# RWKV / delta-rule trunk on one core: layer ends by token half, the norm's scale and offset moved, full-row products

## The reference

```python
for layer in range(2):
    if layer == 0:     # 8 heads of stick-breaking attention (128 wide), 16 RWKV-7 heads (64 wide)
        h = concatenate([attention(...), rwkv7_group(...)]) @ ev_w_out
    else:              # gated delta rule, 32 value heads, chunks of 64
        h = gated_deltanet(x @ od_w_in, ...) @ od_w_out
    x = layer_norm(ALPHA * x + h, ln1_g[layer], ln1_b[layer])
    x = layer_norm(ALPHA * x + square(relu(x @ mlp_w1)) @ mlp_w2, ln2_g[layer], ln2_b[layer])

def layer_norm(x, g, b):
    mu, var = mean(x), mean((x - mu)**2)
    return (x - mu) * rsqrt(var + 1e-5) * g + b
```

## Time and profile before

| | |
|---|---|
| median of 3 runs | 2956.7 us (2956.69 to 2959.77) |
| the profiled execution | 2961.85 us |
| its span, first to last instruction | 2960.2 us |
| mean granted clock of PE | 0.993 |
| PE busy | 2903.2 us (98%) |
| PE weight loads busy | 2531.9 us (86%) |
| DVE busy | 1857.0 us (63%) |
| ACT busy | 1446.9 us (49%) |
| read from HBM | 488.89 MB, 166 GB/s over the span |

### The profile page before, as it was taken

How to read it: one execution, slowest core, us unless ns; L and a number is a source line. 1 busy time by engine, 2 the same in 40 slices (tenths; PEclk the granted TensorE clock), 3 DMA queues, 4 the chain that set the end, 5 groups by cost and what they waited for, 6 DMA issues and landing times.

```text
span 2960.2 us, 53673 instructions
## 1 busy us (share of the span) xinstructions
PE 2903.2 (98%) x20900; PEld 2531.9 (86%) x20900; DVE 1857.0 (63%) x2604; ACT 1446.9 (49%) x2248; POOL 14.9 (1%) x31
## 2 busy tenths in 40 slices
PE   8999999899999999999999999999999999999998
PEld 8888897788888888889999988999887888888886
DVE  5777776755555545565677766577767546455556
ACT  5545544344444434435666765466744434344442
POOL 0000000000000000000000000000000000000000
PEclk9999999999999999999999999999999999999999
DMA  7333344465555555544344444544445555555554
GB/s 246 118 117 115 116 125 149 173 218 192 187 191 192 186 191 188 194 157 136 129 143 144 143 136 144 192 136 146 140 178 179 191 192 185 194 190 192 192 186 149
DMA packets 156762, 493.77 MB, mean 167 GB/s; under 512 B 15600, under 2 KB 50416, under 8 KB 155296
## 3 DMA queue, kind: packets, MB, share of 16 engines
q1 hardware_dynamic: 153488, 475.33, 48.2%
q0 software_dynamic: 2800, 14.94, 1.3%
q10 hardware_dynamic: 288, 0.79, 0.1%
HBM read 488.89 MB, written 2.10 MB: 166 GB/s over the span
## 4 chain that ended last, share of the span: by engine, by line
PE 91%; DVE 5%; ACT 2%; issue 1%; DMA 0%; DVEq 0%; ACTq 0%; SPq 0%
PE pp L433 45%; PE mp L433 11%; PE pp L417 8%; PE mp L417 8%; PE pp L419 4%; PE mp L419 4%; DVE wl L1442 1%; PE mp L867 1%; PE mp L836 1%; PE mp L821 1%; PE mp L873 1%; PE mp L813 1%; ACT wh L935 0%; DMA raw<-in_w_dram 0%; PE mp L787 0%
## 5 line engine op out<-in xcount | busy, mean ns | idle before, releaser
L1442 DVE TENSOR_TENSOR wl<-raw,wh 128x1024 fp32r<-128x1024 f32 (+1 forms) x936 | 1100.9, 1183 | 783.2 <-ACT wh L935 782.2
L935 ACT CAST wh<-raw 128x1024 fp32r<-128x1024 f32 (+1 forms) x936 | 944.8, 1018 | 890.8 <-PE pp L433 287.1
L433 PE MATMUL pp<-aT,wh 128*128 128x256 f32 x3680 | 705.1, 292 | 12.1 <-DVE wl L1442 12.1
L433 PEld LDWEIGHTS pp<-aT,wh 128*128 128x128 f32 x3680 | 575.8, 192 | 28.4 <-issue 16.9
L433 PE MATMUL pp<-aT,wl 128*128 128x256 f32 x1840 | 522.0, 284 | 0.0
L417 PE MATMUL pp<-aT,wh 128*128 128x512 f32 x1024 | 365.4, 401 | 0.0
L417 PE MATMUL mp<-aT,wh 128*128 128x512 f32 x1024 | 360.8, 398 | 0.0
L433 PE MATMUL pp<-wh,hTh 128*128 128x512 f32 x896 | 357.5, 399 | 3.0 <-DVE wl L1442 1.5
L433 PEld LDWEIGHTS pp<-aT,wl 128*128 128x128 f32 x1840 | 353.7, 192 | 0.0
L433 PE MATMUL pp<-wh,hTl 128*128 128x512 f32 x896 | 349.8, 390 | 0.0
L433 PE MATMUL pp<-wl,hTh 128*128 128x512 f32 x896 | 349.5, 390 | 0.0
(11 more groups left out here) (323 smaller groups left out, 3082.4 us busy)
## 6 DMA issues: line engine op xcount, KB each, us to landing
raw<-in_w_dram SPq DMA_DIRECT2D x800, 512.0 KB, 3.3
raw<-in_w_dram SPq DMA_DIRECT2D x136, 384.0 KB, 3.5
ws<-in_ln_dram POOLq DMA_DIRECT2D x8, 1024.0 KB, 7.5
xres<-in_x_dram POOLq DMA_DIRECT2D x1, 2048.0 KB, 8.7
out_dram<-xres SPq DMA_DIRECT2D x8, 256.0 KB, 2.0
ws<-in_lora_dram POOLq DMA_DIRECT2D x8, 192.0 KB, 4.4
xres<-in_xt_dram POOLq DMA_DIRECT2D x2, 512.0 KB, 6.7
ws<-in_c_dram POOLq DMA_DIRECT2D x1, 576.0 KB, 6.4
```

The costliest lines, as they stand in the source:

```text
L433: last = mm(o, lhs, rhs, start=opens and m == 0, stop=end and kk == 1 and m == 2, skip_group_check=True)
L935: nc.scalar.copy(wh[:, q % RING, :, 0:width], raw[:, q % LAND, :, 0:width]).then_inc(S("hi_ready"), 1)
L1442: tt(wl[:, q % RING, :, 0:width], raw[:, q % LAND, :, 0:width], f(wh[:, q % RING, :, 0:width]), ALU.subtract).then_inc(S("lo_ready"), 1)
```

## The change

It has four parts.

1. **Layer ends by token half.** `last_panel` on DVE (the former `tail`, generalised) adds and takes the statistics of the last panel for t = 0 as soon as PE has finished that half of the last unit (`ends`, semaphore `tail`), then for t = 1. `new_x` now normalises without scale and offset (one operation for a piece, `ts` with mean and 1/std), the first 512 columns in pieces of 256. The tiles of PE, ACT and DVE are now 256 columns of both token halves (two k-tiles). ACT applies scale and offset as it reads the transposed block, since they are per-partition numbers there (`lnT`, a new small input, loaded by POOL at the start), into the staging `scaled_x` (two halves of `hid`), copies the high part from it, and DVE subtracts for the low part. In the first tile DVE does the odd block (`odd`) and the two k-tiles are handed over singly. PE's first half unit waits for the first k-tile alone.
2. **Late scale and offset of the residual.** `residual` does `xres * lng + lnb` on DVE, in eight pieces of two operations, in later steps of the MLP's first body, or in the gate steps of layer 1. `lng` and `lnb` move to other places in the work space.
3. **Unread products.** `keep_clock` issues 16 products of 256 columns before the first transposes of each layer end and 6 behind the second tile. Nobody reads them.
4. **Tables and shapes.** Out-projection 0 goes 6+2 instead of 7+1, with 24 units under the last `mix0` and 8 behind. L556 uses all 128 rows of `lw` (the others are zero), L677 the full 128 columns of keys, and the rows not wanted are not read.

```diff
-HOPS_GATES = 4 * (4,) + (5,) + 9 * (3,)
+HOPS_GATES = 8 * (2,) + (5,) + 9 * (3,)
-HOPS_MLP = 4 * (2,) + 56 * (1,)
+HOPS_MLP = 64 * (1,)
+HOPS_E = 2 * (1,) + 31 * (2,)
+HOPS_G = 2 * (1,) + HOPS_GATES[1:]
...
+        scaled_x = [r2(hid[:, i * WIDE:(i + 1) * WIDE], a=UK) for i in range(2)]
...
@@ POOL
+            pool.dma_start(lnT[:, :, :, :], lnt.rearrange("p (k s c) -> p k s c", k=3, s=2)).then_inc(S("masks_in"), 16)
...
@@ PE, unit
+                    if ends and j == 0:
+                        last.then_inc(S("tail"), 1)
...
@@ PE, new_x
+                def keep_clock(count):
+                    if k == 2:
+                        pe.wait_ge(S("evacuated"), B_L1 + 1)
+                    for _ in range(count):
+                        mm(pp[0][:, 0:T] if k == 2 else mb[3][:, 0:T], hTh[:, 0, 0:P], hTh[:, 0, :], start=True, stop=True,
+                           skip_group_check=True)
                 def turn(r):
-                    c, t = divmod(r, TT)
-                    pe.wait_ge(S("x_ready"), 8 * (k - 1) + r + 1)
-                    if 8 * k + r >= 12:
-                        pe.wait_ge(S("xlo"), 8 * k + r - 3)
-                    for e in range(4):
-                        last = nc.tensor.transpose(mb[r % 4][:, e * P:(e + 1) * P],
-                                                   xres[:, t, (4 * c + e) * P:(4 * c + e + 1) * P], ident)
+                    if r >= 4:
+                        pe.wait_ge(S("xhi"), 9 * k + r - 3)
+                    for t in range(TT):
+                        if r >= 2 or t == 0:
+                            pe.wait_ge(S("x_ready"), 18 * (k - 1) + (4 + 2 * (r // 2) if r >= 2 else r + 1))
+                        else:
+                            pe.wait_ge(S("x_ready"), 18 * (k - 1) + r + 3)
+                        for e in range(UK):
+                            bank = mb[2][:, 0:T] if r == 0 and e else mb[r % 4][:, e * T:(e + 1) * T]
+                            last = nc.tensor.transpose(bank[:, t * P:(t + 1) * P],
+                                                       xres[:, t, (UK * r + e) * P:(UK * r + e + 1) * P], ident)
                     last.then_inc(S("xT" if r < 7 else "x_transposed"), 1)
-                for y, tiles in enumerate((range(0, 4), range(4, 6), range(6, 8), ())):
-                    for r in tiles:
-                        turn(r)
-                    pe.wait_ge(S("xlo"), 8 * k + 2 * y + 2)
+                keep_clock(16)
+                turn(0)
+                turn(1)
+                keep_clock(6)
+                for y in range(UNITS + 1):
+                    if 0 < y <= 6:
+                        turn(y + 1)
+                    pe.wait_ge(S("xlo"), 9 * k + y)
                     yield
...
@@ PE, mix0
-                mm(mb[0][:, T:2 * T], lw[0:32, 2, :], loT[0:32, 2, :], start=False, stop=True,
+                mm(mb[0][:, T:2 * T], lw[:, 2, :], loT[:, 2, :], start=False, stop=True,
...
-                            last = mm(mb[0][half(1 - hf), 0:P], KR[:, hf, 0, t, :], st_in, start=True, stop=True,
-                                      skip_group_check=True)
+                            turned_keys = KR[:, hf, :, :, :].rearrange("p w t c -> p (w t c)")[:, t * HC:t * HC + P]
+                            last = mm(mb[0][:, 0:P], turned_keys, st_in, start=True, stop=True, skip_group_check=True)
...
-            drive(late(blocks(P_OUT0, B_OUT0, "A", H, (0, 1, 0, 1), WIDE, per=7), 6, "mix0_out", GROUPS - 1), 28, 0,
-                  mix0(GROUPS - 1, False), HOPS0Z)
+            drive(blocks(P_OUT0, B_OUT0, "A", H, (0, 1, 0, 1), WIDE, per=6), 24, 0, mix0(GROUPS - 1, False), HOPS0Z)
             pe.wait_ge(S("mix0_out"), GROUPS)
-            drive(blocks(P_OUT0, B_OUT0 + 4, "A", H, (0, 1, 0, 1), WIDE, per=1, u0=28, k0=14), 4, 28)
+            drive(blocks(P_OUT0, B_OUT0 + 4, "A", H, (0, 1, 0, 1), WIDE, per=2, u0=24, k0=12, ends=31), 8, 24)
...
@@ ACT, new_x
+                def part(r, e):
+                    c = UK * r + e
+                    return go(scaled_x[r % 2][:, e, :], mb[r % 4][:, e * T:(e + 1) * T], ACT.Identity,
+                              scale=lnT[:, k - 1, 0, c:c + 1], bias=lnT[:, k - 1, 1, c:c + 1])
+                def high(r):
+                    y = scaled_x[r % 2]
...
+                    if r >= 2:
+                        act.wait_ge(S("xlo"), 9 * k + r - 1)
+                    st(part(r, 0))
+                    if r:
+                        st(part(r, 1))
+                    st.settle()
+                    if r == 0:
+                        nc.scalar.copy(aTh[:, 0, :], y[:, 0, :]).then_inc(S("xhi"), 1)
+                        act.wait_ge(S("x_odd"), k)
+                        nc.scalar.copy(aTh[:, 1, :], y[:, 1, :]).then_inc(S("xhi"), 1)
+                        return
+                    nc.scalar.copy(aTh[:, UK * r:UK * r + UK, :], y).then_inc(S("xhi"), 1)
...
@@ DVE, new_x
+                def norm(t, lo, hi):
+                    o = xres[:, t, lo * T:hi * T]
+                    ts(o, o, mv[:, t, 0:1], rstd[:, t:t + 1], ALU.subtract, ALU.mult).then_inc(S("x_ready"), 1)
+                def odd():
+                    dve.wait_ge(S("xT"), 7 * (k - 1) + 1)
+                    ts(scaled_x[0][:, 1, :], mb[2][:, 0:T], lnT[:, k - 1, 0, 1:2], lnT[:, k - 1, 1, 1:2],
+                       ALU.mult, ALU.add).then_inc(S("x_odd"), 1)
+                    dve.wait_ge(S("x_odd"), k)
...
+                dve.wait_ge(S("ln_rstd"), TT * (k - 1) + 1)
+                norm(0, 0, 1)
+                norm(0, 1, 2)
+                dve.wait_ge(S("ln_rstd"), TT * k)
+                norm(1, 0, 1)
+                norm(1, 1, 2)
+                norm(0, 2, 4)
+                odd()
+                low_one(0)
+                norm(1, 2, 4)
+                low_one(1)
+                low(1)
+                yield
+                for r in range(2, UNITS):
+                    if r < 4:
+                        norm(0, 2 * r, 2 * r + 2)
+                        norm(1, 2 * r, 2 * r + 2)
+                    low(r)
+                    yield
+                yield
+            def residual(k, per):
+                for r in range(8):
+                    c, t = divmod(r, TT)
+                    cols = slice(c * WIDE, (c + 1) * WIDE)
+                    o = xres[:, t, cols]
+                    if r == 0:
+                        dve.wait_ge(S("x_transposed"), k)
+                    st(tt(o, o, lng[:, cols], ALU.mult))
+                    st.settle()
+                    tt(o, o, lnb[:, cols], ALU.add).then_inc(S("x_ready"), 1)
+                    if r % per == per - 1:
+                        yield
...
-                body(0, True, False, then(new_x(2 * k + 1), 56))
+                body(0, True, False, then(new_x(2 * k + 1), 6, residual(2 * k + 1, 1), 42))
```

More of the change, by code:

```diff
@@ L393, in to_tiles, with unit @@
                 pe.sem_inc(S("tiles"), 1)
-            def unit(n, u, mode, act, buf, width, ks, first=None, end=False, half=None, ready=None):
+            def unit(n, u, mode, act, buf, width, ks, first=None, end=False, half=None, ready=None, ends=False):
                 ah, al = act
@@ L434, in unit, with blocks @@
                                       skip_group_check=True)
+                    if ends and j == 0:
+                        last.then_inc(S("tail"), 1)
                 if half != 0:
                     last.then_inc(S("unit_used"), 1)
-            def blocks(n, b, mode, act, bufs, width, per=UNITS, u0=0, k0=0, lag=2):
+            def blocks(n, b, mode, act, bufs, width, per=UNITS, u0=0, k0=0, lag=2, ends=None):
                 def one(u, half=None):
@@ L443, in one @@
                     unit(n, u, mode[j % len(mode)], act, bufs[j], width, (k0 + 2 * q, k0 + 2 * q + 1),
-                         first=b + (j + 3 - (lag if j == 0 else 2)) if q == 0 else None, end=q == per - 1, half=half)
+                         first=b + (j + 3 - (lag if j == 0 else 2)) if q == 0 else None, end=q == per - 1, half=half,
+                         ends=u == ends)
                 return one
@@ L727, in body @@
                         unit(n, u + 4 * UNITS, "A", H, j, WIDE, (2 * q, 2 * q + 1),
-                             first=b + (4 + j + 1) if q == 0 else None, end=q == UNITS - 1, ready=ready)
+                             first=b + (4 + j + 1) if q == 0 else None, end=q == UNITS - 1, ready=ready,
+                             ends=over and u == 4 * UNITS - 1)
                     if late:
@@ L920, in _ @@
             pe.wait_ge(S("mix1_out"), 16)
-            drive(blocks(P_OUT1B, B_OUT1B + 4, "A", H, (0, 1, 0, 1), WIDE, per=2, u0=24, k0=12), 8, 24)
+            drive(blocks(P_OUT1B, B_OUT1B + 4, "A", H, (0, 1, 0, 1), WIDE, per=2, u0=24, k0=12, ends=31), 8, 24)
             mlp(P_MLP1, B_MLP1, 3)
@@ L1478, in new_x @@
-                yield
-                for r in range(4, 6):
-                    norm(r + 2)
-                    low(r)
+                def norm(t, lo, hi):
```

(25 more changed lines are left out.)

93 lines of the change are left out of this document (44 added, 49 removed).

## The result

Six runs of the changed kernel have a median of 2941.57 us (2940.32 to 2947.63), six of the kernel before beside them 2959.14 us: ratio 0.9943, interval 0.9932 to 0.9955. The kernel is 17.6 us faster (0.57%). I had said 2932.6 us in a range of 2927 to 2941: the direction was right, the gain was 17.6 instead of 24.1 us, and the time lies just outside the range.

The account below looks back on a forecast made before the run. TensorE's own product stream was taken as the bound, interrupted at three layer ends. 16.2 - 2.4 + 6.5 + 1.4 + 1.9 + 0.5 = 24.1 us off 2961.85 gave 2937.7, less 5.15 made 2932.6 us; range 2927 to 2941.

Parts of the forecast that it names:

- The hole after the change: Three layer ends: by token halves and 256-column pieces, first product at about S + 5.6; 16.2 us gained, 2.4 lost to transposes.
- At nothing: Moved residual scale and offset, ACT's early steps, POOL's extra load and the earlier MLP 0 broadcast: no cost.
- Clock: Behind the three layer ends: unread products hold the granted clock, so following products run at full speed; +6.5 us.
- Rival (a): Layer ends: the clock falls anyway at some or all of them; 2934.5 to 2939.1 us, chance 0.20.
- Rival (b): Layer ends: longer chain or following tiles trickling in, 1 to 2.5 us more each; 2935.6 to 2940 us, chance 0.12.
- The prediction's -1.47: Layer 1 up to its last product: the prediction's terms falling in that stretch, a change of -1.47 us.
- Out-projection 0 as 6+2: Last four units of out-projection 0: two units a block remove PE's waits for DVE's residual add; +1.4 us.
- Rival (e): Out-projection 0: its thin mixer steps show, up to 10.9 us back; 2935 to 2943 us, chance 0.03.
- Full-row products: Layer 0, eight groups: full-width L677 gains 1.9 us; full-row L556 mostly lost to L562's wait, 0.5 us.
- I take the same difference off: Last step: profiled execution lay 5.15 us above the runs' median 2956.7, so 2937.7 becomes 2932.6 us.
- (c): Later tiles at layer ends serialise between ACT and DVE, 2.8 us for each of 18; about 2983 us, chance 0.04.
- (d): Layer ends: PE starts early but waits for its second and third pair; gain under 6 us, 2951 to 2957, chance 0.04.

Follow-up runs that it names:

- the late broadcast: Changed kernel, with the broadcast of the norms' scales and offsets started only when the first and third layer ends are over; 2937.96 us, ratio 0.9931.
- a whole first tile: On the late broadcast, ScalarE does both blocks of each layer end's first tile, with one copy and one low part; corrected rerun 2939.37 us, ratio 0.9932.
- the spread one: On the late broadcast, VectorE's twelve convolution steps of layer 1's first head group divided into three parts with splits between; 2938.41 us, ratio 0.9928.
- both old products: Changed kernel with layer 0's lora product (L556) back to 32 rows and its turned-state product (L677) back to 64 columns; 2946.31 us.
- the lora product alone old: Changed kernel with only layer 0's lora product (L556) back to 32 rows, the turned-state product kept full width; 2941.81 us.

## Why the prediction was right or wrong

**The hole after the change.** The chain of 5.6 us was right: 5.69 at the second end, 5.62 to 5.63 at all three with the late broadcast, and the 1.0 us expected for a whole first tile came out as 1.0 (6.62). Its steps hold one by one, so this is not errors that cancel. At the first end with the late broadcast (S is 556.91) the first add starts at S - 0.87 (foretold -0.95), the statistics of the halves end at S + 0.85 and 2.42 (0.8 and 2.5), ACT's scaling begins at S + 4.04 (4.1), its copy ends at S + 5.04 (5.05) and the low part at S + 5.57 (5.5). What failed is its starting point at the first end, and with it the term (11.36 - 5.6): it was 2.85, not 5.76. The step reads "DVE may start the first half's add at S - 0.95"; at that end DVE was free at S + 1.65. I had counted the new chain from PE's products alone and checked DVE's queue only for the division 6+2.

**At nothing: the broadcast.** "The broadcast of scale and offset for MLP 0 starts earlier, with eight units to land in" is the sentence that was wrong, and it is the cause of the former. I asked whether the transfer lands in time, not what it takes from the weight stream that shares the queues. Undone alone, it gives the 2.9 us of the first hole, 0.4 of the third and 3.6 in all. This part is shown. By the ratios against the kernel before (0.9931 and 0.9940) the 3.6 us are within the intervals; the holes, the waits and the medians beside each other on one chip are what shows it.

**Clock.** Right as a mechanism: without the unread products the loss is 6.8 us (+6.5 predicted). At the first end it fell all the same, since the late DVE left 3.20 us of nothing. That cost about 0.6 us behind the hole (two pairs at 0.64 instead of 0.35) and 0.4 in it: of the 2.89 us that this hole is over 5.62, the add's delay from S - 0.87 to S + 1.65 is 2.52. Under the low clock the unread products do delay something: the low part was ready at 565.31, and the first product started behind them, at 565.68. Rival (a) thus came true at one end of three, for a reason that it did not name. Rival (b), a longer chain, did not: the chain is 5.62.

**A clock dip outside the holes.** Behind the stall in layer 1 the clock fell to 0.50 in this trace, though not in that of before:

```profile
1370.00:1372.00 2.00, 2.00 (x12) 2.00 (x11) 2.00 (x4) 1.94 (x3) 0.00 (x0) 0.50 0.83 262
```

It is worth 1.0 us: where it held here layer 1 took 926.39 to 926.43 us (four traces with the old stall, one with the spread one); where it fell, and had held behind the second end, 927.35 to 927.50 (five traces). The prediction's -1.47 would be 926.32. The stall of 2.4 us is the same in the nine with the old stall and in the kernel before, so nothing here ties the dip to the change; what decides it stays open.

**Out-projection 0 as 6+2.** The term of 1.4 us came in but for one wait of 0.3 us that is left in the changed kernel, and not from the division: with 7+1 the stalls are gone too. The same edit also has VectorE's add of a finished block stand one step earlier in its order (wait=1 in the hook behind the mixer); in the trace of before a split stood ahead of that add. That this is what removed them fits both traces and was not tried alone. The division's own worth, 3.0 us of hole and 0.75 ahead of it, I had left out as a gain, though my working says that DVE is just free with 6+2. Rival (e), thin mixer steps, gave nothing: the last product came earlier than predicted.

**Full-row products.** L677 (now L707) some 2.7 us instead of 1.9 (from POOL's first load to the last product of out-projection 0 it takes 489.26 us with both old products and 486.53 with the lora product alone old). L556 (now L584) costs 0.47 extra, not 0.27, and gave 0.4 in place of 0.5, in the first group; its wait grew by 0.38 us a group in six groups, as foretold. Of the 5.24 us gained ahead of the first hole, 0.28 stand before POOL's first load, where traces of the changed code differ by 1.2 us. The next period has 0.73, the five after it 1.73, and the stretch behind the seventh load 2.50. That last stretch is 2.33 shorter than before with both old products too, and the waits for the add, 1.4 before and none there, are part of it; the rest, about 0.9 us, has no cause that I showed.

**Sum and offset.** 24.1 was foretold against the profiled execution, which gave 20.2; with the late broadcast it gives 23.5 (2961.85 to 2938.36). The forecast of 2932.6 was 9.0 us low. 3.9 of these are the sum: 2.9 at the first hole, 0.45 at the third, 1.2 and 1.1 in layer 1 and MLP 1, less 1.8 that came in above the terms elsewhere. The other 5.1, the larger part, are the last step, "I take the same difference off": three runs of before had their median 5.15 below the profiled one, six have it 2.7 below (2959.14), and after the change the two agree within 0.1. A difference between one execution and three is scatter, and I carried it as if it belonged to the kernel. With 2.7 in its place the prediction would have read 2935.0; with none, 2937.7. The time lies only 0.6 us outside the range, but that closeness says little: MLP 1 alone scatters by 3.5 us over the traces. The terms say where the prediction failed.

Rivals (c), serialising tiles, and (d), a wait for the second or third pair, did not occur: PE waits for no low part behind the first.

## What to carry to other kernels

When a chain is shortened, ask of every engine in it not only how long its link takes but when its queue is free for the first one; here one late engine took half of the gain at one of three places. A transfer that starts earlier is not free because it lands in time: look at what streams beside it, and start it when that stream has slack. A difference between a profiled execution and the median of three runs is no constant; give it to the range, not to the sum.

## What the runs showed of the hardware

Fourteen traces with three layer ends each give 42 holes, which can be ordered by the longest stretch in which PE had nothing. At 2.95 us or more the granted clock went to the lower level all 13 times, also with the 22 unread products around it. At 2.47 to 2.59 us it did 4 times in 5. At 1.47 us or less it did once in 24, and that one was without the six products behind the transposes. Behind the stall of 2.4 us in layer 1, the same in twelve traces of the changed code, it fell eight times and held four times; in the one trace of the kernel before it held. So for an idle time near 2.5 us these traces have both outcomes and show no cause for either, and one trace is one draw.

Two broadcasts of 1024 KB to all partitions beside a stream of 512 KB weight tiles held the DMA queues at a share of 1.01 and 378 to 395 GB/s for 10 us, and one weight tile came 5.51 us late for ACT, which with the broadcast moved waited only for PE in this stretch.
